# mLSTM and linear recurrence merged into one stage of a two-block transformer kernel

## The reference

```python
qk_m = silu(causal_depthwise_conv(qk_m, mlstm_conv)); q_m, k_m = split(qk_m, 2)
i_pre = 15 * tanh((i_m + i_bias) / 15);  f_pre = 15 * tanh((f_m + f_bias) / 15)
g = cumsum(log_sigmoid(f_pre))                      # per head
# h_t = sum_s exp(g_t - g_s + i_s - m_t) (q_t.k_s / 8) v_s / max(|sum_s ...|, exp(-m_t)),  m_t the running maximum
y_mlstm = sigmoid(o_m) * rms_norm_per_head(h) * mlstm_norm

# linear recurrence, per head: S_t = S_{t-1} diag(w_t) + (S_{t-1} a_t) b_t^T + v_t k_t^T,  y_t = S_t r_t
y = group_norm(y) * ln_w + ln_b + sum(r * k * r_k) * v
y_rwkv = y * (sigmoid(xg) @ g_up)
```

## Time and profile before

| | |
|---|---|
| median of 3 runs | 3215.77 us (3215.07 to 3219.16) |
| the profiled execution, its own time | 3219.56 us |
| its span, first to last instruction | 3217.8 us |
| TensorE busy, instructions | 3079.1 us (96%), 17718 |
| VectorE busy | 1389.7 us (43%) |
| ScalarE busy | 1109.9 us (34%) |
| mean granted clock of TensorE over the span | 0.961 |

### The profile page before, as it was taken

How to read it: one execution, slowest core, us unless ns; L and a number is a source line. 1 busy time by engine, 2 the same in 40 slices (tenths; PEclk the granted TensorE clock), 3 DMA queues, 4 the chain that set the end, 5 groups by cost and what they waited for, 6 DMA issues and landing times. The chain is left out here.

```text
span 3217.8 us, 41971 instructions
## 1 busy us (share of the span) xinstructions
PE 3079.1 (96%) x17718; PEld 2593.0 (81%) x17718; DVE 1389.7 (43%) x1909; ACT 1109.9 (34%) x1568; POOL 13.9 (0%) x25
## 2 busy tenths in 40 slices
PE   8999999888999999999999888999999989999998
PEld 7888788677888888888888667888878878888887
DVE  3333445545333254333345546333346157545642
ACT  3322334323222245222334423222235245434431
POOL 0000000000000000000000000000000000000000
PEclk9999999688999999999999878999999989999999
DMA  3333311002133332233411102123342200213322
GB/s 132 99 98 110 124 41 61 17 5 99 40 98 96 108 124 72 92 98 116 137 32 61 33 5 85 35 92 98 111 137 85 66 25 29 65 60 98 98 93 85
DMA packets 71482, 254.48 MB, mean 79 GB/s; under 512 B 8056, under 2 KB 9208, under 8 KB 71296
## 3 DMA queue, kind: packets, MB, share of 16 engines
q1 hardware_dynamic: 71296, 251.81, 24.3%
HBM read 249.68 MB, written 2.10 MB: 78 GB/s over the span
## 5 line engine op out<-in xcount | busy, mean ns | idle before, releaser
L206 PE MATMUL ps<-h_hi,w_space 128*128 128x512 f32 (+3 forms) x5440 | 1515.5, 364 | 17.4 <-DVE h_lo L304 17.2
L206 PEld LDWEIGHTS ps<-h_hi,w_space 128*128 128x128 f32 x5440 | 981.2, 190 | 181.3 <-DVE h_lo L304 20.7
L194 DVE TENSOR_TENSOR w_space<-w_raw,w_space 128x1024 fp32r<-128x1024 f32 x440 | 536.2, 1225 | 1081.1 <-ACT w_space L187 1080.5
L206 PE MATMUL ps<-h_lo,w_space 128*128 128x512 f32 (+3 forms) x2720 | 985.6, 362 | 0.0
L187 ACT CAST w_space<-w_raw 128x1024 fp32r<-128x1024 f32 x440 | 457.8, 1047 | 991.4 <-PE ps L206 591.1
L216 PE MATMUL ps<-w_space 128*128 128x512 f32 x3312 | 769.2, 394 | 16.6 <-DVE w_space L194 15.8
L216 PEld LDWEIGHTS ps<-w_space 128*128 128x128 f32 x3312 | 627.4, 190 | 148.8 <-issue 12.7
L206 PEld LDWEIGHTS ps<-h_lo,w_space 128*128 128x128 f32 x2720 | 516.1, 190 | 78.8 <-issue 1.4
L582 ACT CAST w_space<-act_p 128x512 fp32r<-128x512 f32 x88 | 54.6, 621 | 187.4 <-DVE act_p L594 172.4
L597 DVE TENSOR_TENSOR w_space<-act_p,w_space 128x512 fp32r<-128x512 f32 x88 | 61.0, 693 | 69.8 <-ACT w_space L582 69.8
L594 DVE TENSOR_TENSOR act_p<-act_s,ps 128x512 f32<-128x512 f32 x88 | 60.0, 681 | 71.3 <-PE ps L206 71.3
(11 more groups left out here) (382 smaller groups left out, 2441.7 us busy)
## 6 DMA issues: line engine op xcount, KB each, us to landing
w_raw<-in_w_ffn_in SPq DMA_DIRECT2D x176, 512.0 KB, 3.6
w_raw<-in_w_ffn_out SPq DMA_DIRECT2D x88, 512.0 KB, 3.6
w_raw<-in_w_in SPq DMA_DIRECT2D x64, 512.0 KB, 3.7
w_raw<-in_w_up SPq DMA_DIRECT2D x44, 512.0 KB, 3.6
w_raw<-in_w_out SPq DMA_DIRECT2D x24, 512.0 KB, 3.6
w_raw<-in_w_down SPq DMA_DIRECT2D x22, 512.0 KB, 3.6
w_raw<-in_w_ple_gate SPq DMA_DIRECT2D x16, 512.0 KB, 4.9
gain_pre<-in_gains_pre SPq DMA_DIRECT2D x10, 512.0 KB, 5.1
```

The source lines that it names most:

```text
L194: nc.vector.tensor_tensor(self.lo(n), self.raw[:, n % SLOTS, :], self.hi(n).bitcast(F32), ALU.subtract).then_inc(self.lo_ready, 1)
L206: m = nc.tensor.matmul(c.ps[:, bank, t], part[:, cols], moving[:, k, t], start=(k == 0 and i == 0), stop=(k == KD - 1 and i == 2))
```

## The change

Both stages become one, `recurrence_stage`. Head h of the mLSTM goes beside tile t = h of the recurrence: between the rounds of the inverse stands one step of the head on each engine, and the sums of head h stand in the first round of tile h + 1. There is one barrier less in a layer, one clearing of semaphores less, and one opening in which both parts' preparations stand in one order. PSUM is shared: the recurrence's products go to banks 0 to 4 instead of eight banks, the mLSTM has one bank each for the scores, the maximum and the sums, so a step's scores wait for the weighing of the step before, and a head's sums for the `normalise` of the head before. `weight` is written in place of `below`, `weighted_s` has one buffer instead of two. q and k lie in `c.proj[:, 0:4]`, in place of attention tiles that are no longer needed. The roots of the mLSTM are taken in two pairs of heads. In the last stage 13 semaphores are declared there that were global before. All other lines are moved only.

The order of the work, TensorE:

```diff
+                pe.wait_ge(padded, 2)
                 turn(0)
+                values_by_token()
                 pairs_of_a(0)
-                pe.wait_ge(loaded, 32)
+                pe.wait_ge(loaded, 48)
                 for j in range(2):
-                    nc.tensor.matmul(c.ps[:, 6 + j, :], g_up[:, j * P:(j + 1) * P], mix[:, G_AT, :], start=True,
+                    nc.tensor.matmul(c.ps[:, j, :], g_up[:, j * P:(j + 1) * P], mix[:, G_AT, :], start=True,
                                      stop=True).then_inc(gate_done, 1)
+                a_values(0)
+                pe.wait_ge(u_ready, 1)
+                columns_of(MAX_BANK, u, u_turned)
+                pe.wait_ge(gate_ready, 2)
                 pairs_of_r(0)
-                a_values(0)
                 for t in range(NT):
-                    more = t + 1 < NT
+                    more, h = t + 1 < NT, t
                     square(t, 1)
-                    if t >= 2:
-                        turn_back(t - 2)
                     if t:
                         local(t - 1)
                         steps_of_state(t - 1)
+                        sums(h - 1)
+                    spread_max(h)
                     square(t, 2)
                     inverse(t, 1)
+                    if t >= 2:
+                        turn_back(t - 2)
+                    if t == 0:
+                        pe.wait_ge(low_ready, 1)
+                        pe.wait_ge(v_copied, 2)
+                        columns_of(SUM_BANK, low, low_turned)
                     if more:
                         turn(t + 1)
+                    scores(h, 0)
                     square(t, 3)
                     inverse(t, 2)
                     if t:
                         next_state(2 * t - 2)
+                    scores(h, 1)
                     square(t, 4)
                     inverse(t, 3)
                     if t:
-                        outputs(t - 1)
                         next_state(2 * t - 1)
                     if more:
                         pairs_of_a(t + 1)
+                    scores(h, 2)
+                    if t:
+                        outputs(t - 1)
                     square(t, 5)
...
-                turn_back(NT - 2)
                 local(NT - 1)
                 steps_of_state(NT - 1)
+                sums(M_HEADS - 1)
+                turn_back(NT - 2)
                 next_state(NCH - 2)
                 outputs(NT - 1)
+                heads_back(1)
                 turn_back(NT - 1)
```

ScalarE and VectorE, the new opening and the loop (ScalarE):

```diff
                 rows_of(0)
+                act.wait_ge(biased, 2)
+                nc.scalar.activation(g_tanh[:, :, :], c.gates[0:4, :, :], ACT.Tanh, scale=1.0 / CAP).then_inc(act_chain, 1)
...
+                nc.scalar.activation(soft, soft, ACT.Ln, bias=1.0).then_inc(softened, 1)
...
+                act.wait_ge(u_turned, 1)
+                nc.scalar.copy(u_col[:, :, :], c.ps[:, MAX_BANK, 0:NT * M_HEADS]).then_inc(u_copied, 1)
+                for t in QK_ORDER:
+                    nc.scalar.activation(qk[:, t, :], qk[:, t, :], ACT.Silu).then_inc(qk_ready, 1)
+                for j in range(2):
+                    nc.scalar.activation(o_gate[:, j, :], o_gate[:, j, :], ACT.Sigmoid).then_inc(o_ready, 1)
                 for t in range(NT):
+                    h = t
                     powers(t, 1)
...
                     if t + 1 < NT:
                         rows_of(t + 1)
-                    for i in range(3, STEPS + 1):
-                        powers(t, i)
+                    weights(h, 0)
+                    powers(t, 3)
+                    weights(h, 1)
+                    powers(t, 4)
...
                     if t:
                         squares(t - 1)
+                    solution(t)
+                    if t:
                         root(t - 1)
-                    solution(t)
+                    if t == 2:
+                        head_roots(0)
```

```diff
+                dve.wait_ge(softened, 1)
+                ch.link(nc.vector.tensor_tensor_scan(low, soft, soft, 0.0, ALU.add, ALU.max))
+                nc.vector.scalar_tensor_tensor(out=u, in0=g_tanh[:, 0, :], scalar=CAP, in1=low, op0=ALU.mult,
+                                               op1=ALU.add).then_inc(u_ready, 1)
                 masks_of_a(0)
+                dve.wait_ge(u_ready, 1)
+                nc.vector.tensor_tensor_scan(run_max, u, u, NEG, ALU.max, ALU.max).then_inc(max_ready, 1)
+                a_values(0)
```

More of the change, by code:

```diff
@@ L688, in first_part @@
         elif MQ_T <= n:
-            m = nc.scalar.activation(c.y[:, M_QK + n - MQ_T, :], bank, ACT.Copy, scale=self.tap(0, n))
+            m = nc.scalar.activation(c.proj[:, QK_AT + n - MQ_T, :], bank, ACT.Copy, scale=self.tap(0, n))
         else:
@@ new lines, in columns_of, with spread_max @@
+                def columns_of(bank, rows, done):
+                    for n in range(NT):
+                        m = nc.tensor.matmul(c.ps[:, bank, n * M_HEADS:(n + 1) * M_HEADS], rows[:, n * P:(n + 1) * P],
+                                             c.mats[0:4, MATS.index("ident"), 0:4], start=True, stop=True)
+                    m.then_inc(done, 1)
+                def spread_max(h):
+                    if h == 0:
+                        pe.wait_ge(max_ready, 1)
+                        pe.wait_ge(u_copied, 1)
+                    else:
+                        pe.wait_ge(below_ready, NT * h)
+                    nc.tensor.matmul(c.ps[:, MAX_BANK, :], select[:, h, :], run_max, start=True, stop=True).then_inc(max_spread, 1)
@@ new lines, in _ @@
+                act.wait_ge(act_chain, 1)
+                nc.scalar.activation(soft, soft, ACT.Exp, scale=-CAP).then_inc(act_chain, 1)
+                act.wait_ge(act_chain, 2)
+                nc.scalar.activation(soft, soft, ACT.Ln, bias=1.0).then_inc(softened, 1)
+                for i in range(2):
+                    act.wait_ge(v_turned, i + 1)
+                    nc.scalar.copy(v_tok[:, 2 * i:2 * i + 2, :, 0:DH],
+                                   c.ps[:, (SCORE_BANK, SUM_BANK)[i], :].rearrange("p (n h d) -> p n h d", n=2, h=M_HEADS)).then_inc(v_copied, 1)
@@ L2101, in _ @@
                         carry(2 * t - 2)
+                        if t >= 2:
+                            norm(t - 2)
+                        normalise(h - 1)
+                    if t == NT - 1:
+                        head_norm(0)
+                    exponent(h, 0)
                     inverse(t, 1)
@@ L2117, in _ @@
                     inverse(t, 5)
+                    weigh(h, 3)
                     if more:
[L2119 removed]
                         masks_of_r(t + 1)
```

477 lines of the change are left out of this document (206 added, 271 removed).

## The result

| | before | changed |
|---|---|---|
| median of the runs made together | 3217.47 us (3215.07 to 3224.13) | 3173.36 us (3171.87 to 3186.17) |
| span of the profiled execution | 3217.8 us | 3172.1 us |
| TensorE busy | 3079.1 us | 3051.3 us |
| mean granted clock of TensorE, as a share of full speed | 0.961 | 0.974 |

The account below looks back on a forecast made before the run. The kernel was taken as bound by TensorE, at half rate in the mLSTM. The likeliest case, one layer losing 41 us and the other 7, gave 3216 + 48 = 3264 us, range 3172 to 3312.

Parts of the forecast that it names:

- The opening: From the barrier to the second product of the squaring: 24.9 us instead of 81.0, 56.1 saved per layer.
- The clock at that point: TensorE's clock as the loop begins: about 3 us idle before the masks, then short work; 0.50 from the power copy on.
- The loop at full clock: Merged loop with TensorE at clock 1.00: 139.3 us a layer with the opening, against 167.3, so 28 us saved.
- It fits: VectorE's work in a tile of the merged loop at full clock: 20 us in 25.
- the forecast's five terms: Full-clock times in a layer: tile 0 16 us, tiles 1 to 3 25, 27.4 and 25.5, end 20.5.
- Does it come back?: Clock's return at the ten transposes of tile 2's third pass: even odds per layer; then 174 us, 7 lost.
- the merged loop is made of just the shapes that did not: Main point on the merged loop: busy is not enough to bring the clock back, and its product shapes had not.
- the loop at half clock: Merged loop with TensorE at 0.50: 208 us a layer with the opening, 41 us lost (33 to 60).
- a return in the third tile: Clock rises in tile 2: 174 us a layer, 7 lost; in both layers 3230 us, chance 0.16.
- The rival of an early return: Clock returns in the loop's first two tiles: 3190 to 3220 us, chance 0.10.
- The rest: Buffer move of q and k and moved semaphores: nothing; narrower PSUM hidden at half clock, otherwise within the waits.
- the table load: Exp and Sqrt table changes in the loop: 1.28 us each, in tiles 2 and 3 before a power copy TensorE awaits.

Follow-up runs that it names:

- the fill: Changed kernel with unread 64x64 products (80, 24 and 20) in three waits of TensorE in the opening; 3159.96 us, ratio 0.9819 against the kernel before.
- moved wait: Changed kernel with TensorE's wait for GpSimd's memsets moved from ahead of the transposes to ahead of the loop; 3167.55 us.
- moved waits and fill together: Changed kernel with memset wait and sigmoid moved later, tanh and exp ahead of the row copies, 64x64 products in four waits; 3147.51 us.
- thin fill: Changed kernel with unread products of 4 rows by 4 columns (12, 4 and 3) in three waits of the opening; 3177.2 us.
- fill in the kernel before: Kernel before the change, with 60 unread 64x64 products ahead of the mLSTM's columns and 64 ahead of its first scores; 3223.31 us.

## Why the prediction was wrong

- **The opening** was right: 25.1 us against 24.9, with the second squaring at 616.6 against 616.4 and ScalarE's silu, sigmoid and loads as what it waits for. The second's agreement is partly luck: the dense stage ended 1.3 us later than in the trace of before, and the chain behind it was 1.1 us shorter, most of it in `a_values` and the columns, 1.7 us (608.23 to 609.93) and not 2.6, at a clock that was up. That 56.1 us were "saved" by it was a matter of where the cut lay: 41.9 of them were the heads, which the loop takes up again.
- **The clock at that point** was right in its result, 0.50 from the power copy on. That choice between 0.50 and 1.00, on which the 24 us for tile 0 rest, was the author's estimate, and the runs showed more moves on the way: the clock had risen at 603.5, fallen at 610.4 behind the wait for the masks, risen at 613.8 behind `pairs_of_r` and the first squaring, and fallen again at 617.2 behind the wait of 1.53 us for the power copy. Tile 0 took 20.1 us.
- **The loop at full clock** was right, but it was put on the wrong case: the first layer of the fill shows the forecast's five terms within 1 us each. (The 11.5 us of a head in them are a quarter of the 20.6, 18.1 and 7.5 us of the earlier trace rows.) "It fits" for VectorE holds: TensorE stands between 0 and 2.1 us in a tile.
- **"Does it come back?" is the step that failed**, with "the merged loop is made of just the shapes that did not". It put 208 us on the layer for the loop at half clock, or 174 with a return in the third tile; the runs showed a return within tile 0, in both layers, and 145.4. The forecast had three stretches at half clock without a rise, and one of them, 662.1 to 665.4 with transposes and pairs, was taken to show that 64x64 products can't raise the clock. In the changed kernel it rises at 603.5 behind the same two kinds of products, before the gates, and in tile 0 behind squarings. In its second layer it has risen before the first pair, behind nothing but sixteen transposes, where the kernel before has eight in a row (timeline of the changed kernel; 48 pairs take 2.47 us at half clock):

```profile
1804.95 1.97 PE L1518 MATMUL ps<-mats,proj 128*128 128x128 f32 x8 [6.30 <-POOL rec_r_prime L1505]
1806.71 1.89 PE L1663 MATMUL ps<-mats,proj 128*128 128x128 f32 x8
1808.53 1.44 PE L1527 MATMUL ps<-proj 64*64 64x64 f32 x48
```

  The moved wait shows the same in its first layer (clock 1.00 from 598.3, the first pair at 598.48). One stretch without a rise had shown only that it had not risen yet. The squarings of before, from 670.68, ran at full clock already (1.00 from 668.8), so its trace held no case of them at half; the fill shows by itself that 64x64 products raised it, from 0.50 to 1.00 at 595.9, 3.1 us behind its start. The right entry was "not seen", between both ends, and not "does not".
- **The rival of an early return** named the right mechanism at 0.10, and its price was too high: with the forecast's own terms, and tile 0 halfway between its 16 and 24, a rise within tile 0 gives 24.9 + 20 + 25 + 27.4 + 25.5 + 20.5 = 143.3 us, 24 saved a layer, 3168 us. A rise within tile 1 (25 to 45 for it, and 24 for tile 0) gives 3176 to 3216, so the 3190 to 3220 answer to a rise late in tile 1.
- **The rest**: the table load cost 1.3 us of waiting in tile 2, as forecast, though in front of a weight and not of a power copy; that tile is over its 27.4 by the two falls alone (26.6 with the fill). Against the fill's layer, half clock costs the changed kernel 4.5 us in tile 0 and 3.0 in tile 2, 7.3 in the layer's sum; the kernels' medians differ by 13.4.

## What to carry to other kernels

When a forecast hangs on whether the clock comes back, count what the trace shows of each kind of product at half clock, and treat a kind that it never shows there as open in both directions. A stage whose own products leave TensorE at clock 0.50, as the heads did (609.3 to 651.2 before), can gain from being put between products at 1.00: here that, more than the saved opening, made the 44 us of the merge. And where TensorE must wait at such a border, unread products in the wait can pay, if they are of a kind that has been seen to raise the clock: fill of 64x64 alone gave 13 us, fill of 4 rows none, and moved waits and fill together 26. When two cuts of two kernels are compared, check first that they start at the same instruction and hold the same products.

## What the runs showed of the hardware

- TensorE busy with 4-row products for the whole of 5.1 us stayed at clock 0.50 (593.1 to 598.2, thin fill), and with 64x64 products in the same wait the clock rose to 1.00 before the wait was over (595.9, fill of 64x64); the scores of the mLSTM's first head lost the raised clock (0.50 from 621.6, behind waits of 0.22, 0.55 and 0.58 us, fill in the kernel before), and sums, scores and maxima behind them ran at 0.50 (622 to 660).
- Sixteen 128x128 transposes in a row, and nothing else, brought TensorE's clock from 0.50 to 1.00 (1804.95 to 1808.4 in the changed kernel, 594.97 to 598.3 with the moved wait); eight in a row did not (654.28 to 656.2 and 661.24 to 663.1 before).
- The clock fell from 1.00 to 0.50 behind a stretch in which TensorE never stood, the sums and the maximum (it fell at 668.4, in the stretch 665.5 to 668.8 of the changed kernel): not only waiting loses it.
- Where the clock moves in the loop, the two layers of one execution can differ: from the dense stage's last transposes to the first product behind the stage they take 150.9 and 145.8 us with the moved wait, 156.5 and 144.2 with the thin fill, 141.3 and 144.0 with the fill, and 171.6 and 171.6 in the kernel before. So the places of the falls vary within one kernel. That this makes the scatter of its runs (3158.7 to 3172.8 us for the moved wait) is likely but not shown: the kernel before, whose clock moves at the same places in both layers, also spread over 3215.0 to 3228.3 in one set.
